# A two-layer attention network on one core: GpSimd instead of VectorE scales the probabilities, and splits its weight units in between

## What is computed

```python
s = einsum('...gnqd,...nkd->...gnqk', qb, kc) * SCALE      # plus mask, bias or log counts
m = max(s, axis=-1)
p = exp(s - m[..., None])
den = sum(p, axis=-1)                                       # in one case + exp(sink - m)
o = einsum('...gnqk,...nkd->...gnqd', p, v) / den[..., None]
```

## Time and profile before

| | before |
|---|---|
| median of three runs | 1079.36 us |
| profiled execution | 1080.68 us |
| its span | 1078.8 us |
| busy: TensorE, VectorE, ScalarE, GpSimd | 90, 61, 45, 17% |
| mean granted TensorE clock | 0.938 |
| attn0, attn1, attn2, attn3 begin near | 107, 466, 828, 1007 us |

### The profile page before, as it was taken

The page is one execution under the profiler, slowest core; times in us unless marked ns, Lnnn a source line. Parts: engine busy times, 40 slices in busy tenths (PEclk is TensorE's granted clock), DMA queues, the critical chain, the costliest instruction groups (busy, mean ns, idle before and its releaser), DMA issues. The chain is left out here.

```text
span 1078.8 us, 15064 instructions
## 1 busy us (share of the span) xinstructions
PE 969.0 (90%) x5804; PEld 818.0 (76%) x5804; DVE 662.0 (61%) x1097; ACT 483.2 (45%) x891; POOL 179.9 (17%) x129
## 2 busy tenths in 40 slices
PE   5995878899999999988899999998998789886778
PEld 4794546799998888855699999886886468676556
DVE  5697783555556468646455565546871857867672
ACT  5362552455455345345344455434542635343550
POOL 2003020000000000131000000003654300407540
PEclk9996888899999999988989999998998999898899
DMA  8481002365566656510536656656852025443001
GB/s 317 131 257 75 1 1 79 115 198 176 177 211 199 189 167 210 176 59 1 156 118 194 196 158 204 214 168 158 256 173 78 1 64 176 147 140 134 1 1 39
DMA packets 96791, 148.71 MB, mean 138 GB/s; under 512 B 6272, under 2 KB 59680, under 8 KB 96592
## 3 DMA queue, kind: packets, MB, share of 16 engines
q1 hardware_dynamic: 94512, 140.50, 41.0%
q10 hardware_dynamic: 1296, 4.83, 1.3%
q0 software_dynamic: 912, 2.41, 1.0%
HBM read 146.67 MB, written 1.05 MB: 137 GB/s over the span
## 5 line engine op out<-in xcount | busy, mean ns | idle before, releaser
L889 DVE TENSOR_TENSOR w_lo<-w_raw,w_hi 128x1024 fp32r<-128x1024 f32 (+2 forms) x230 | 272.8, 1210 | 152.4 <-ACT w_hi L600 148.7
L600 ACT ACTIVATE w_hi<-w_raw 128x1024 fp32r<-128x1024 f32 (+2 forms) x269 | 273.5, 1042 | 169.6 <-DMA w_raw<-in_w_gate_up 74.7
L1466 PE MATMUL ps<-hT_hi,w_lo 128*128 128x256 f32 x832 | 240.1, 289 | 8.1 <-POOL w_lo L492 4.6
L1467 PE MATMUL ps<-hT_hi,w_hi 128*128 128x256 f32 x832 | 239.4, 288 | 0.0
L1468 PE MATMUL ps<-hT_lo,w_hi 128*128 128x256 f32 x832 | 239.2, 287 | 0.0
L1466 PE MATMUL ps<-w_hi,hT_lo 128*128 128x512 f32 (+3 forms) x448 | 173.7, 388 | 8.1 <-DVE w_lo L889 4.4
L1466 PEld LDWEIGHTS ps<-hT_hi,w_lo 128*128 128x128 f32 x832 | 163.9, 197 | 9.4 <-issue 6.5
L1468 PE MATMUL ps<-w_lo,hT_hi 128*128 128x512 f32 (+3 forms) x448 | 170.7, 381 | 0.0
L1467 PE MATMUL ps<-w_hi,hT_hi 128*128 128x512 f32 (+3 forms) x448 | 170.5, 381 | 0.0
L1467 PEld LDWEIGHTS ps<-hT_hi,w_hi 128*128 128x128 f32 x832 | 163.9, 197 | 0.0
L1468 PEld LDWEIGHTS ps<-hT_lo,w_hi 128*128 128x128 f32 x832 | 163.9, 197 | 0.0
(11 more groups left out here) (213 smaller groups left out, 1192.8 us busy)
## 6 DMA issues: line engine op xcount, KB each, us to landing
w_raw<-in_w_gate_up SPq DMA_DIRECT2D x176, 256.0 KB, 4.4
w_raw<-in_w_down SPq DMA_DIRECT2D x44, 512.0 KB, 4.4
w_raw<-in_w_in_e SPq DMA_DIRECT2D x38, 512.0 KB, 5.1
w_raw<-in_w_qkv_o SPq DMA_DIRECT2D x24, 512.0 KB, 3.8
w_raw<-in_w_in_o SPq DMA_DIRECT2D x20, 512.0 KB, 3.6
w_raw<-in_w_out_e SPq DMA_DIRECT2D x16, 512.0 KB, 4.6
w_raw<-in_w_out_o SPq DMA_DIRECT2D x16, 512.0 KB, 3.5
w_raw<-in_w_in_e SPq DMA_DIRECT2D x8, 268.0 KB, 2.7
```

Source lines behind the costliest of these rows:

```text
L600: n.activation(w_hi[:, u % RING, 0:size], w_raw[:, u % RING, 0:size], ACT.Copy).then_inc(hi_ready, 1)
L889: v.tensor_tensor(w_lo[:, u % RING, 0:size], w_raw[:, u % RING, 0:size], w_hi[:, u % RING, 0:size].bitcast(F32), ALU.subtract).then_inc(lo ...
L1466: m.matmul(o, lhs[1], rhs[0], start=start, stop=False)
L1467: m.matmul(o, lhs[0], rhs[0], start=False, stop=False)
```

## The change

`scale_probs` on VectorE ends with the factor and signals `fac_ready`. A new loop on GpSimd waits for it, does the two multiplications and signals `probs_ready`. In the same loop, at odd steps from 5 on, GpSimd takes its weight units: in attn0 one per odd step, units 0 to 7 at steps 5 to 19. In the other stages `first` is -5, so at step 5 `k` is 4 and the call covers units 0 to 4; units 5, 6 and 7 follow at steps 7, 9 and 11. The loop over all 8 units that stood ahead of the stage's other work is gone. In attn3, the squares, power and gating product move into the loop too, at steps 9, 13 and 15. The norm semaphores are shared between norms by an offset, which changes names and counts, not the order of work.

```diff
-        def split(which):
-            for u in range(*POOL_UNITS[which]):
+        def split(which, lo=0, hi=None):
+            for u in list(range(*POOL_UNITS[which]))[lo:hi]:
                 pool.wait_ge(hi_ready, u + 1)
...
+        def attention(stage, at_step=None):
+            inst, i0 = INST[stage], INST0[stage]
+            first = 3 if stage == "attn0" else 3 - 2 * AHEAD
+            for s in range(len(inst) + LAG + 5):
+                j = s - 1
+                if 0 <= j < len(inst):
+                    i, w = i0 + j, P if inst[j]["causal"] else T
+                    pool.wait_ge(fac_ready, i + 1)
+                    g.tensor_scalar(prob[:, i % 3, 0:w], prob[:, i % 3, 0:w], fac[:, i, 0:1], None, ALU.mult)
+                    g.tensor_scalar(prob[:, i % 3, 256:512], prob[:, i % 3, 256:512], fac[:, i, 1:2], None, ALU.mult)\
+                     .then_inc(probs_ready, 1)
+                if s >= 5 and s % 2:
+                    k = (s - first) // 2 - 1
+                    split(stage, k if s > 5 else 0, min(k + 1, RING))
+                if at_step:
+                    at_step(s)
...
-        split("attn0")
+        attention("attn0")
...
-        split("attn1")
+        attention("attn1")
...
-        split("attn2")
+        attention("attn2")
...
-        split("attn3")
-        for hf in range(2):
-            pool.wait_ge(mix_hi, PAIR0["attn3"] + 2 * hf + 2)
...
+        def sub_norm(s):
+            if s in (9, 13):
+                hf = (s - 9) // 4
+                pool.wait_ge(mix_hi, PAIR0["attn3"] + 2 * hf + 2)
+                if hf == 0:
+                    link(g.memset(ones, 1.0))
+                link(g.tensor_tensor(od_sq[:, hf, :], odp[:, hf, :], odp[:, hf, :], ALU.mult))
+                pool.sem_inc(sem("od_sq"), 1)
+            if s == 15:
+                pool.wait_ge(sem("od_ms"), 1)
+                g.tensor_tensor(od_rstd, od_rstd, halfs[:, 0:8], ALU.pow).then_inc(sem("od_rstd"), 1)
+                g.tensor_tensor(odp, odp, gd, ALU.mult).then_inc(sem("od_gated"), 1)
+        attention("attn3", sub_norm)
...
-            link(v.reciprocal(fac[:, i, :], den[:, i, :]))
+            ins = v.reciprocal(fac[:, i, :], den[:, i, :])
             if "gate" in it:
                 h, br = it["gate"]
-                link(v.tensor_tensor(fac[:, i, :], fac[:, i, :], gates[:, :, h, br], ALU.mult))
+                link(ins)
+                ins = v.tensor_tensor(fac[:, i, :], fac[:, i, :], gates[:, :, h, br], ALU.mult)
...
-            w = P if it["causal"] else T
-            v.tensor_scalar(prob[:, i % 3, 0:w], prob[:, i % 3, 0:w], fac[:, i, 0:1], None, ALU.mult)
-            v.tensor_scalar(prob[:, i % 3, 256:512], prob[:, i % 3, 256:512], fac[:, i, 1:2], None, ALU.mult)\
-             .then_inc(probs_ready, 1)
+            ins.then_inc(fac_ready, 1)
```

More of the change, by code:

```diff
@@ L256, in net, with norm_sem, norm_at @@
     H1, HT, KC, VC, CS = 2, 1, 6, 7, 2
+    NORM_ORDER = {0: 0, 1: 1, 2: 2, 3: 3, 5: 4, 6: 5}
+    NORM_EVENTS = {"ss": 4, "ms": 2, "rstd": 2, "h": 4}
+    def norm_sem(what, k):
+        return sem(f"norm4_{what}" if k == 4 else f"norm_{what}")
+    def norm_at(what, k):
+        return 0 if k == 4 else NORM_ORDER[k] * NORM_EVENTS[what]
     slot_full = [sem(f"slot_full_{s}") for s in range(RING)]
@@ L267, in net @@
     scores_ready, max_ready, exp_ready = sem("scores_ready"), sem("max_ready"), sem("exp_ready")
-    probs_ready, pv_done = sem("probs_ready"), sem("pv_done")
+    fac_ready, probs_ready, pv_done = sem("fac_ready"), sem("probs_ready"), sem("pv_done")
     mix_prod, mix_hi, mix_lo = sem("mix_prod"), sem("mix_hi"), sem("mix_lo")
@@ L493, in split @@
                                 w_hi[:, u % RING, 0:size].bitcast(F32), ALU.subtract).then_inc(pool_lo, 1)
+        def attention(stage, at_step=None):
[14 more added lines that the diff above has]
+                    at_step(s)
         def norm_power(k):
             for t in range(NT):
-                pool.wait_ge(sem(f"norm{k}_ms"), t + 1)
+                pool.wait_ge(norm_sem("ms", k), norm_at("ms", k) + t + 1)
                 g.tensor_tensor(rstd[:, t:t + 1], ms[:, t:t + 1], halfs[:, 0:1], ALU.pow)\
-                 .then_inc(sem(f"norm{k}_rstd"), 1)
+                 .then_inc(norm_sem("rstd", k), 1)
         link(g.memset(halfs, -0.5))
@@ L606, in load_gain @@
             if wait is not None:
-                act.wait_ge(sem(f"norm{wait}_h"), 4)
+                act.wait_ge(norm_sem("h", wait), norm_at("h", wait) + 4)
             act.dma_start(gb[:, :] if dst is None else dst, src.partition_broadcast(P))\
@@ L615, in square @@
             n.activation(hA[:, t, cols], x[:, t, cols], ACT.Square, scale=D ** -0.5,
-                         accum_out=ss[:, 2 * t + c:2 * t + c + 1]).then_inc(sem(f"norm{k}_ss"), 1)
+                         accum_out=ss[:, 2 * t + c:2 * t + c + 1]).then_inc(norm_sem("ss", k), 1)
         def high(k, t):
@@ L804, in _ @@
             for c in range(2):
-                square(5, t, c, sem("norm4_h"), 2 * t + c + 1)
+                square(5, t, c, norm_sem("h", 4), 2 * t + c + 1)
             if t == 0:
@@ L893, in stats @@
         def stats(k, t, eps, pieces):
-            dve.wait_ge(sem(f"norm{k}_ss"), pieces)
+            dve.wait_ge(norm_sem("ss", k), norm_at("ss", k) + pieces)
             v.scalar_tensor_tensor(out=ms[:, t:t + 1], in0=ss[:, 2 * t:2 * t + 1], scalar=eps,
                                    in1=ss[:, 2 * t + 1:2 * t + 2], op0=ALU.add, op1=ALU.add)\
-             .then_inc(sem(f"norm{k}_ms"), 1)
+             .then_inc(norm_sem("ms", k), 1)
         def scale(k, t, q, dst=None, g=None):
-            dve.wait_ge(sem(f"norm{k}_rstd"), t + 1)
+            dve.wait_ge(norm_sem("rstd", k), norm_at("rstd", k) + t + 1)
             if t == 0 and q == 0:
@@ L907, in scale @@
                                    scalar=rstd[:, t:t + 1], in1=(gb if g is None else g)[:, cols],
-                                   op0=ALU.mult, op1=ALU.mult).then_inc(sem(f"norm{k}_h"), 1)
+                                   op0=ALU.mult, op1=ALU.mult).then_inc(norm_sem("h", k), 1)
         def low(k, fill):
@@ L1234, in _ @@
             if t == 0:
-                dve.wait_ge(sem("norm4_h"), 2)
+                dve.wait_ge(norm_sem("h", 4), 2)
                 norm_first(5, EPS_2, 2)
-        dve.wait_ge(sem("norm4_h"), 4)
+        dve.wait_ge(norm_sem("h", 4), 4)
         norm_second(5, EPS_2)
@@ L1450, in norm_tile @@
             for q in range(2):
-                pe.wait_ge(sem(f"norm{k}_h"), 2 * t + q + 1)
+                pe.wait_ge(norm_sem("h", k), norm_at("h", k) + 2 * t + q + 1)
                 f = FILL[f"norm{k}"] + 2 * t + q
```

10 lines of the change are left out of this document (2 added, 8 removed).

## The result

The changed kernel takes 1142.37 us (median of 4 runs, 1136.09 to 1146.46) against 1078.63 for the kernel before; the ratio is 1.058, 95% interval 1.052 to 1.064. The forecast was 1102, range 1083 to 1121: the direction was right, the size was not. The profiled execution has a span of 1137.7 us against 1078.8, so 58.9 us more where the sum had 22.8.

What follows compares the result with a forecast made beforehand. The prediction took TensorE to set the pace in dense parts, and in attention stages its transposes to wait 42.0 us for VectorE's scaling. Terms summed to +22.8 on 1080.7, giving 1103.5, or 1102 on the median's footing; range 1083 to 1121.

Steps and rivals of the forecast that it cites:

- GpSimd scales: Attention stages: scaling on GpSimd lengthens the chain by 0.20 us in 20 pairs and 0.37 in 16, +9.9 us.
- its own work in attn3: attn3: second squaring delays TensorE's step 13, +2; power and gating product precede the last scaling, +3.4; together +5.4 us.
- five at one go: Step 5 of attn1, attn2, attn3: TensorE waits 8.7, 9.3 and 11.2 us while GpSimd takes five units, +29.2 us.
- clock, inside the others: TensorE's granted clock: +9 us after the three stalls, -10 given back elsewhere, net -1 (-15 to +6).
- Held-up rotations: Ahead of attn0: four VectorE instructions no longer held by GpSimd's units, 11.3 us down to 3.0, -8.2 us.
- Held-up instructions in the stages: Attention stages: VectorE's L1061, L1057 and L1020 no longer held by GpSimd's units, all on the chain, -19.3 us.
- Single units: Units between even and odd scalings in the stages: GpSimd late by 0.4 us for 17 units, +6.8 us.
- Slow scaling: Rival: GpSimd's scaling runs at L575's rate, term +26.2 instead of +9.9, 1118 us; chance 0.16.
- Quick scaling: Rival: GpSimd's scaling runs at the fill's rate, term -4.8, single units hardly late, 1085 us; chance 0.11.
- no change: Rival: the five-unit stall is half hidden (-15) and the scaling is quick, 1079 us; chance 0.07.
- faster: Rival: GpSimd's passes fit beside the scores, so all 42.0 us of TensorE's transpose wait go, 1069.5 us; chance 0.08.

Runs made afterwards that it cites:

- experiment 6: The kernel before, with GpSimd's 32 weight units of the four stages moved to VectorE: 1062.46 us, ratio 0.984.
- experiment 9: The changed kernel with all 32 stage units and attn3's squarings and gating product on VectorE, GpSimd keeping the scaling and one power: 1103.96 us.
- experiment 4: The changed kernel with the 32 output projection units of the four stages on VectorE: 1107.26 us.
- experiment 1: The changed kernel with units 0 to 3 of attn1, attn2 and attn3 taken ahead of the stage again, one unit at step 5: 1112.77 us.
- Experiment 13: The changed kernel with each GpSimd multiplication cut to 32 columns in causal stages and 80 in the others, the rest left unscaled: 1100.96 us.
- experiment 12: The kernel of experiment 9 with GpSimd scaling the even instances only and VectorE the odd ones: 1088.76 us.
- experiment 11: The kernel of experiment 9 with VectorE making the odd instance's factor ahead of the next maximum: 1074.78 us.
- experiment 2: The changed kernel with the scaling back on VectorE and GpSimd's units where the change puts them: 1095.09 us, ratio 1.013.
- experiment 8: The changed kernel with 32 identity products added on TensorE while it waits at step 7 of attn1 and attn2: 1142.79 us.

## Why the prediction was wrong

Six medians stand in a grid: who takes the units, and when, against who scales.

| units | VectorE scales | GpSimd scales |
|---|---|---|
| on VectorE | 1062.5 | 1107.3 |
| GpSimd, four ahead of the stage | 1079 to 1082 (before) | 1112.8 |
| GpSimd, five at step 5 | 1095.1 | 1142.4 (after) |

From the kernel before to the changed one a path leads over experiments 6, 9, 4 and 1, and each of its steps answers to terms of the sum (the steps add up to 62.1, which is 1142.37 less the 1080.29 of before beside experiment 6):

| step | measured | in the sum |
|---|---|---|
| before to 6, and 4 to 1: GpSimd's units off the stages, and back as single units | -17.8, +5.5: -12.3 | -8.2 - 19.3 + 6.8: -20.7 |
| 6 to 9: GpSimd scales | +41.5 | +9.9 |
| 9 to 4: its own work in attn3 | +3.3 | +5.4 |
| 1 to after: five at one go | +29.6 | +29.2 |
| clock, inside the others | | -1 |

The steps of 3.3 and 5.5 lie within the spread of the runs on either side: attn3 takes 52.2 us in experiment 9 and 52.0 in experiment 4. The kernel before moved between 1078.6 and 1082.4 from one group of experiments to another, so a step is known to a few microseconds at best.

*The step that failed* is "For the passes no row is the operation alone ... I take the copy's, since it reads, writes and has this size", with 0.72 and 0.95 us an instance. It measures 1.50 and 1.82, above even the upper bound of 1.11 and 1.48 that I took from L575. By the prediction's own formula the term would have been 20 x (1.50 + 0.12 - 0.64) + 16 x (1.82 + 0.12 - 0.70) = 39.4 us, so 29.5 of the 36.1 us missed in the profiled execution. Experiment 13 is the test: with passes of the assumed size the forecast comes true.

*A second step failed beside it*, and the sum hides it: "The even instance's scaling runs beside the scores and costs nothing, unless GpSimd is late with it." In the stages with two passes of 256 columns GpSimd is late with it. When it scales the even instances alone, the kernel is 26.3 us over experiment 6 (experiment 12), and in the wide stages of experiment 9 even transposes wait 18.8 us where they waited 4.5. That 41.5 came out so near the formula's 39 is in part luck: its four stages miss their shares by up to 7.6 us, in both directions. In the changed kernel itself the waits are mostly where the prediction had them: 70.0 us ahead of odd instances, the three stalls included, and 10.7 ahead of even ones (21.0 and 8.8 before).

The upper bound failed because I scaled L575's 1024 columns down in proportion. Passes of 32, 80, 128 and 256 columns take 362, about 485, 604 and 924 ns, so a pass is 0.28 us plus 2.5 ns a column, and with 1024 columns that gives 2.84, an estimate; L575 is 2.95. Only the fixed part was missing: spread over 2.88 ns a column, it vanished. The argument against the slow case, that "two-input work on 1024 columns takes 2.37 us a piece, and one input should not cost more", was wrong: the scaling of 1024 columns costs more than that unit.

*Held-up rotations*: -8.2 was forecast and 11.4 us are won ahead of attn0, with TensorE's wait at 2.93 where "about 3" was said. *Held-up instructions in the stages*: -19.3, "all on the chain", was probably too much; no run separates it. Experiment 6 gets 17.8 for this and the rotations together, and VectorE pays for its own units out of that; in the changed kernel some are still held, L1090 on 128x2 elements among them. *Single units*: by the 5.5 above right in size, as far as that can be told. The *five units* were right in place, number and cost (waits of 31.8 us where 29.2 was forecast).

The total of experiment 13 hides errors that cancel. Cut as above, it takes 99.4, 52.9, 300.6, 45.6, 318.3, 47.5, 136.9, 60.5 and 36.3 us. attn1 and attn2 lose 4.3 and 5.5 where the stall alone was put at 8.7 and 9.3, and attn3 loses 25.1 where the stall and GpSimd's own work come to 16.6. There, in the changed kernel, TensorE's sixteen small products (L1880), now behind the second squaring, stand ahead of the next scores. I had +2 for it, and VectorE then idles 8.71 us. How much of this is the wait and how much the clock behind it, no run separates.

*The notes.* The prediction set the Trainium skill (GPSIMD Engine Reference, Engine selection: one-input operations roughly at line rate) beside L575. These runs decide against it for this instruction: 924 ns for 256 columns, where VectorE takes 0.35 us.

*The rivals.* "Slow scaling" (1118) was the right mechanism at too small a size. "Quick scaling", "no change" and "faster" are out, the last because its transposes do wait. But experiment 11 shows the point that "faster" turned on: with the factors early the passes mostly hide. The 1079 of "no change" was a slip as well: 1102 less 15 and less 14.7 is 1072.

## What to carry to other kernels

When the cost of an operation is taken from another size, split the row into a fixed part and a part per column before scaling it, and let the range reach past the only row of that very operation. Before moving an elementwise pass to a slower engine, ask where its input becomes ready: here the same passes cost 41.5 us behind the next maximum, and 13 ahead of it. And work inserted "between" two steps comes in one piece where more than one is due.

## What the runs showed of the hardware

GpSimd's multiplication by a per-partition scalar takes 0.28 us plus 2.5 ns a column over 32 to 256 columns (four widths, above), against 0.29 and 0.35 us on VectorE for 128 and 256 columns.

The holding up goes both ways. The trace of before showed VectorE's instructions held until GpSimd's unit ends; with units on VectorE, GpSimd's passes are held too (experiment 12: 1.20 and 1.43 us instead of 0.92). Units in a row hold one instruction of VectorE each, and the copy out of the accumulators goes through (experiment 2: 0.68 us with a unit under way).

Seven microseconds of extra products in a wait kept the granted clock at 1.00 through the wait, and not after it (experiment 8). In attn1 it was 0.50 for the 20.5 us that followed, where without them it was 0.50 for 5.8 us and 0.96 for the next 14.7; in attn2 it was 0.80 with them and 0.81 without.
